# Products of ones with the identity in three waits of TensorE, between the router and the first expert of a hybrid decoder layer

## The reference, cut to what matters

```python
h = rmsnorm(x, norm1_g)
proj = h @ w_in                      # pool input | q | k | v | out-gate | forget-gate
a, new_pool = pool_mixer(...)
b, new_S = gla_mixer(...)            # gated linear attention, state S per sequence
x = x + jnp.concatenate([a, b], axis=-1) @ w_out
x = x + hier_moe(rmsnorm(x, norm2_g), ...)
y = rmsnorm(x, final_g)

# hier_moe: 4 groups of 4 experts; the best group, then the best two experts in it
gprob = softmax(x @ w_rg + b_rg);  gp, gidx = top_k(gprob, 1)
ep, eidx = top_k(softmax(elog[gidx]), 2)
y = sum over experts of combine * ((silu(x @ wg) * (x @ wu)) @ wd)
```

## Time and profile before

| | us |
|---|---|
| median of 3 runs | 877.61 |
| lowest and highest run | 877.37, 878.31 |
| the profiled execution's own time | 879.68 |
| its span, first to last instruction | 877.9 |
| TensorE busy | 845.3 (96%) |
| mean granted TensorE clock | 0.981 of full |

### The profile page before, as it was taken

The page is one execution under the profiler, slowest core; times in us unless marked ns, Lnnn a source line. Parts: engine busy times, 40 slices in busy tenths (PEclk is TensorE's granted clock), DMA queues, the critical chain, the costliest instruction groups (busy, mean ns, idle before and its releaser), DMA issues.

```text
span 877.9 us, 15841 instructions
## 1 busy us (share of the span) xinstructions
PE 845.3 (96%) x5828; PEld 749.4 (85%) x5828; DVE 526.8 (60%) x1237; ACT 383.5 (44%) x734; POOL 244.6 (28%) x272
## 2 busy tenths in 40 slices
PE   6999999999999999998899999999999999999993
PEld 5989879999988787775789988889988999888992
DVE  5537424657778435557585676656666656766573
ACT  7545303656367425544334434344343444433442
POOL 1000000000000110002045654447545555445472
PEclk9999999999999999999599999999999999999997
DMA  9121001102222182336188889978899887898871
GB/s 291 43 97 47 2 0 49 49 1 56 49 96 96 59 274 91 150 145 216 60 275 290 300 304 325 306 271 310 291 310 324 307 288 278 290 360 295 286 256 50
DMA packets 118505, 166.56 MB, mean 190 GB/s; under 512 B 17012, under 2 KB 95928, under 8 KB 118469
## 3 DMA queue, kind: packets, MB, share of 16 engines
q1 hardware_dynamic: 103109, 135.48, 45.7%
q0 software_dynamic: 15360, 30.59, 10.2%
HBM read 146.84 MB, written 41.17 MB: 214 GB/s over the span
## 4 chain that ended last, share of the span: by engine, by line
PE 47%; another core or an unknown queue 1%; ACT 1%; issue 1%; DVE 0%; POOL 0%; ACTq 0%; POOLq 0%
PE bank L1912 31%; PE bank L1922 4%; PE bank L1933 3%; PE bank L1924 3%; PE bank L1923 3%; PE bank L1900 2%; PE bank L1893 1%; ACT split L2012 1%; POOL out L1820 0%; PE bank L1905 0%; DVE wdlo L2116 0%; PE bank L1939 0%; DVE x L2188 0%; ACT hs L2014 0%
## 5 line engine op out<-in xcount | busy, mean ns | idle before, releaser
L1912 PE MATMUL bank<-big,ring 128*128 128x160 f32 x2048 | 286.1, 301 | 0.1
L1912 PEld LDWEIGHTS bank<-big,ring 128*128 128x128 f32 x2048 | 281.9, 191 | 1.4
L1836 POOL TENSOR_TENSOR hold_at<-ident 128x1 f32<-128x1 f32 x63 | 53.1, 842 | 175.3 <-DVE lists L2083 128.4
L2116 DVE TENSOR_TENSOR wdlo<-wdn,split 128x1024 fp32r<-128x1024 f32 x64 | 76.7, 1219 | 0.0
L2008 ACT ACTIVATE sg<-bank 128x160 f32<-128x160 f32 x64 | 19.5, 304 | 109.7 <-PE bank L1912 95.4
L2012 ACT CAST split<-wdn 128x1024 fp32r<-128x1024 f32 x64 | 64.9, 1039 | 0.0
L502 PE MATMUL bank<-split,ring_r 128*128 128x384 f32 (+1 forms) x192 | 64.4, 336 | 0.1
L504 PE MATMUL bank<-split,ring_r 128*128 128x384 f32 (+1 forms) x192 | 61.7, 321 | 0.0
L2111 DVE TENSOR_TENSOR hs<-hid,hs 128x128 fp32r<-128x128 f32 x64 | 18.9, 295 | 57.3 <-ACT hs L2014 46.8
L1922 PE MATMUL bank<-split,hs 128*128 128x512 f32 x128 | 52.6, 411 | 0.0
L1399 PE MATMUL bank<-split,ring_r 128*128 128x512 f32 (+1 forms) x128 | 51.7, 404 | 0.3 <-PEq L1191 0.3
(11 more groups left out here) (390 smaller groups left out, 1788.4 us busy)
## 6 DMA issues: line engine op xcount, KB each, us to landing
wdn<-in_w_down SPq DMA_DIRECT2D x32, 1024.0 KB
ring<-in_w_gate SPq DMA_DIRECT2D x32, 1024.0 KB, 5.4
ring<-in_w_up SPq DMA_DIRECT2D x32, 1024.0 KB
ring<-in_w_in SPq DMA_DIRECT2D x8, 1024.0 KB, 5.9
x<-in_x_prompt SPq DMA_DIRECT2D x8, 512.0 KB, 6.1
h_rows<-h SPq DMA_DIRECT2D x8, 512.0 KB, 2.6
sums<-x SPq DMA_DIRECT2D x8, 512.0 KB, 3.6
v<-in_x_prompt SPq DMA_DIRECT2D x4, 512.0 KB, 5.4
```

The source lines that it names most:

```text
L1836: nc.gpsimd.tensor_tensor(hold_at[:], ident[:, 0:1], ident[:, 1:2], ALU.add).then_inc(e_hold, 1)
L1912: x = nc.tensor.matmul(bank[f % 2][:, side * 256:side * 256 + W], ring[:, u, k, c0:c0 + P], xT[:, k, :], start=k == 0, stop=k == KC - 1)
L2116: nc.vector.tensor_tensor(wdlo[:, k, :], wdn[:, k // 2, (k % 2) * D:(k % 2 + 1) * D], wdhi[:, k, :].bitcast(F32), ALU.subtract).then_inc(e ...
```

## The change

A function `keep_busy(n)` is added to TensorE's stream of `b2_all`. It issues n products of 128x128 by 128x128 in float32, with `onesf` as the stationary and `ident` as the moving operand, into the first 128 columns of bank 4. Nobody reads the result, and no semaphore is waited for or signalled. It is called in three places: 10 products ahead of the wait for `r_m`, 2 ahead of the wait for `rows_0.e_oh`, and 18 behind `states(7)`, at the end of the block. Nothing else is changed; the other engines' streams are the same.

```diff
+        def keep_busy(n):
+
+            for _ in range(n):
+                nc.tensor.matmul(bank[4][:, 0:P], onesf[:], ident[:], start=True, stop=True)
+
         def states(b):
...
         for b in range(3):
             states(b)
+        keep_busy(10)
         pe.wait_ge(r_m, 1)
...
             else:
+                keep_busy(2)
                 pe.wait_ge(rows_0.e_oh, 1)
...
         for b in range(4, DEC_B):
             states(b)
+        keep_busy(18)
```

## The result

The change makes the kernel slower. Four runs take 881.48 to 886.89 us, median 883.64; before, in the same comparison, 877.96 us. The ratio is 1.0068, with a 95% interval of 1.0035 to 1.0101: clear of no change, though less than 1%. Forecast were 874.4 us and a range of 872.9 to 876.9. The profiled execution of after takes 884.36 us with a span of 882.6, 4.7 us more than before's span.

What follows compares the result with a forecast made beforehand. TensorE was taken to bound the kernel, with 20.5 us at half clock around the router's end and first expert. Gains 0.55 + 0.8 + 1.87 = 3.2 us took the 877.61 us median to 874.4 us, range 872.9 to 876.9.

Steps and rivals of the forecast that it cites:

- the first call: Ten products ahead of the rank products: 2.2 us within 2.79 us of idle time, costing nothing at full clock.
- the states: states(4) to states(7) ahead of the block's end: at full clock eight products take 3.6 us, against 7.19 at half.
- The third call: Eighteen products behind the states: 4.0 us at full clock plus the drain, ending at 426.6.
- Rival 2: Clock still falls between 414.7 and 419; eighteen products take 5.9 us: +2.4 us, 880.0 us, up to +6.9; chance 0.10.
- The barrier: At the block's end: it waits for TensorE's products to finish, so the added ones are last there.
- Transposes and copies: Behind the barrier: TensorE's ten transposes and ScalarE's copies at full clock gain 0.8 us, bounds 0.5 and 1.24.
- The first sixteen: First expert's sixteen gate and up products: 4.35 us at full clock instead of 6.22, gaining 1.87 us, the largest term.
- rival 1: Clock falls late, between last added product and first gate and up product: gain 0.55 to 1.7 us, about 876.5; chance 0.22.
- The sum: Whole gain from block end, transposes with copies, and first gate and up products: 0.55 + 0.8 + 1.87 = 3.2 us.
- The block end term: Block before the barrier ends at 426.6 instead of 427.13, 0.55 us earlier, with TensorE's added products last.
- The other bound of the term: If TensorE's sequencer passes the barrier while products run, VectorE is last at 425.3 and the gain is 1.8 us.
- Transposes and the clock: Behind the barrier: if transposes don't count as busy, 4.0 us are one stretch and the clock may fall there.

Runs made afterwards that it cites:

- half-row run: The changed kernel with its thirty added products over 64 of the 128 rows: 886.07 us, ratio 1.0115 against the kernel before.
- those with eight: Changed kernel with early products in the last router tile, two behind each of states(4) to states(7), none ending the block; with six after the barrier: 876.92 and 875.00 us.
- hold: Changed kernel plus four early products, four ahead of the one-hot matrix's first half, four behind each of states(4) to states(7), no final eighteen: 877.98 us, ratio 1.0004.
- its repeat: The changed kernel run again, unchanged: 885.93 us, ratio 1.0070 against the kernel before.
- the kernel with nine: The kernel before with only nine added products at the end of the block, instead of eighteen: 879.68 us, ratio 1.0018.
- the six: Six more products at the start of the last block, ahead of the step number reads; added to hold: 876.77 us, ratio 0.9988.
- spread: Changed kernel plus four early products in the last router tile's waits and four behind each of states(4) to states(7), no final eighteen: 885.07 us, ratio 1.0087.

## Why the prediction was wrong

The failed step is one assumption, made twice: that the clock is full when TensorE comes to the added products, at the first call and again at the states and the third.

- **The step that failed first** is the first call: "the cost is nothing as long as the clock is full, as it is up to 414.73". I took the place of the fall from one execution. In after it came at 410.3, behind 2.9 us with 1.32 us of TensorE work; five of eight traces with that stretch as before had it at 409.6 to 412. I had named the case and priced it at 3.5 us (measured 2.75, 4.0 and 4.2 us), but put it in the tail, because "no row shows this". The thin stretch ahead of 409 was in the trace that I had; I read only the gap that ended in the fall. From before:

```profile
407.12 0.46 PE L1351 MATMUL bank<-ident,x 64*128 64x64 f32 x4 [0.71 <-DVE x L1563]
...
408.87 0.29 PE L1377 MATMUL bank<-es,big 128*64 128x20 f32 x2 [0.35 <-DVE big L1540]
```

- **The states**: "eight take 3.6 us" is right at full clock (3.72 us). That the clock is full behind them was assumed; in after they began with it and lost it, behind the thin stretch from 419 to 422. And once it was lost they didn't bring it back: the earlier trace rows had shown 7.2 us of them at 0.50, which I used only in weighing the transposes. The half-row run bears it out: their 64 rows are enough to explain it.
- **The third call**: this is the larger loss. I took 4.0 us at full clock, an end at 426.6 and a block that ends 0.55 us earlier; in after the products took 5.68 us, in part at half clock, and the transposes start 5.64 us later. Rival 2's mechanism and deciding point were right (the eighteen outlast the block at half clock), and its 5.9 us for them. With a fall at 414.7 to 419 I gave +2.4 us to +6.9 and 880.0 us; the eighteen alone cost 3.8 us by the ratio, inside these bounds but above the likeliest. The place of the fall was wrong for after, which falls ahead of that stretch and again behind it. The mistake is the chance: 0.10.
- **The barrier** waits for TensorE's products: right (products end at 433.50, the 1.63 us of issue begin at 433.75).
- **Transposes and copies**, 0.8 us: 0.83 in after. **The first sixteen**, 1.87 us: not in after, where rival 1 came on top (a fall at 437.6 behind idle time and transposes, 6.13 us against 6.06 before). With the clock held it is 1.6 us (431.20 to 435.66 against 431.92 to 437.98); I had subtracted a piece of the chain (4.35 us) from a duration of the timeline (6.22), where the timeline has 4.61 us at full clock.
- **The sum**, 3.2 us for a clock that holds: reached with other products in other places (3.1 and 3.3 us at the landmark, 2.6 permille or 2.3 us by the ratio). That they agree is luck. The block end term, 0.55 us, was mis-sized: the kernel that holds with sixteen behind the states is later by 0.65, those with eight earlier by 0.7 to 0.9, and no kernel has the eighteen at the end and a clock that holds. An estimate for that one, from the trace without products behind the states (they end 8.55 us behind `Mb`), 4.2 us for the eighteen with their drain and 1.89 us to the transposes as in after: 14.6, or 0.1 us earlier than before. The states don't start 0.3 us earlier at full clock (4.82 us behind `Mb` in hold, 4.85 in before), and they take 3.72. With 0.8 and 1.6 us that makes 2.5 us in place of 3.2, which would still have been a gain. The other bound of the term, 1.8 us, was too large as well: 0.8 us is what is left when no product is last.
- **Transposes and the clock.** In after, its repeat and the kernel with the eighteen alone the clock fell in or right behind the transposes. The Trainium skill (TensorE: Matmul & The Clock Gate, Part 4: PE-mode transpose) says that a transpose doesn't count as busy for the clock in the way that a product does. The runs don't separate them from the 1.9 us of idle time ahead: with the eighteen alone the fall came at 434.8, 0.2 us into the transposes, so there they had hardly run; and in hold and in the kernel with nine, with the same idle time and transposes, the clock stayed at 1.00. In the four traces in which the clock was full at the barrier and the six stood behind it, it didn't fall there. That a transpose doesn't count is neither shown nor excluded.

## What to carry to other kernels

In these runs, products that only keep TensorE's clock up were free where three things held: they lay in an idle stretch, that stretch was long enough even at half clock or the clock held up to it, and nobody waited at its end for TensorE. So cover the first thin stretch ahead of a critical one first, a product or two in each wait, and put few products or none ahead of a barrier. Before such a change take several traces of the same kernel: where the clock falls differs from one execution to the next, and a fall that costs nothing today is not seen in the times.

## What the runs showed of the hardware

- Dense products over 64 of 128 rows didn't bring the clock back from 0.50 in 15 us (state products and eighteen of ones by the identity, 425.86 to 433.74); over 128 rows the same eighteen did, in each of the three traces (after 2.9, 2.9 and 5.6 us). State and added products mixed half and half kept a full clock (hold, 419 to 427), and didn't bring back a low one (spread, 419 to 436).
- Ones by the identity, with 127 of 128 moving values zero, brought the clock back (after, from 0.50 to 1.00 at 430.8, under products only).
- Four added products between state products take 1.09 us at full clock (hold, 419.66 to 420.75), more than the 0.89 us of four in a long row.
- The same stream loses the clock at different places in different executions. Of the seven traces with this stretch as in before and no half-row products, five have the fall within 0.5 us of the start of `states(0)` (409.6 to 412.0, as the stream itself starts earlier or later) and two 5.7 us behind it (414.3 and 414.7). So the fall comes at one of two places, both behind a stretch with little work.
- The times of before hide it: its runs beside the experiments are 876.67 to 884.71 us, wider than the three first runs (877.37 to 878.31).
